# A gate row spread over partitions through DRAM instead of on TensorE, and a wait for the keys' second half moved to the third pass

## What is computed

```
mod = c_act @ w_ada[l] + b_ada[l]
shift1, scale1, gate1, shift2, scale2, gate2 = jnp.split(mod, 6, axis=-1)
...
merged = g_pool * (pooled @ w_branch_pool[l]) + g_attn * (attn @ w_branch_attn[l])
x = x + gate1[:, None, :] * (merged @ w_out[l])
h2 = modulate(x, norm_ffn_g[l], shift2, scale2)
x = x + gate2[:, None, :] * peer_ffn(h2, peer_wq[l], peer_sub_keys[l], peer_u[l], peer_v[l])
...
# second block, forgetting_attention
logits = jnp.einsum('bhqd,bhkd->bhqk', qb, k).astype(jnp.float32) * scale
logits = logits + cb[..., :, None] - cum[..., None, :]
p = jax.nn.softmax(logits, axis=-1)
```

## Time and profile before

| | us |
|---|---|
| median of 3 runs | 1173.78 |
| lowest, highest | 1173.57, 1175.6 |
| the profiled execution | 1174.26 |
| its span, first to last instruction | 1172.4 |
| PE busy | 1041.2 (89%) |
| DVE busy | 826.7 (71%) |
| ACT busy | 423.2 (36%) |
| POOL busy | 290.3 (25%) |

### The profile page before, as it was taken

How to read it: one execution, slowest core, us unless ns; L and a number is a source line. 1 busy time by engine, 2 the same in 40 slices (tenths; PEclk the granted TensorE clock), 3 DMA queues, 4 the chain that set the end, 5 groups by cost and what they waited for, 6 DMA issues and landing times.

```text
span 1172.4 us, 13740 instructions
## 1 busy us (share of the span) xinstructions
PE 1041.2 (89%) x5066; PEld 702.4 (60%) x5066; DVE 826.7 (71%) x1912; ACT 423.2 (36%) x895; POOL 290.3 (25%) x262
## 2 busy tenths in 40 slices
PE   5999999898999996886886878788899999999997
PEld 3799976644555543432332323333389878999986
DVE  5699765768767768778887555555566878888843
ACT  3545622322332222222222111111266665665631
POOL 0000001444354543353544444445000000000000
PEclk8999999999999998898988999989999999999999
DMA  9977594999999999899999999999994443554530
GB/s 367 427 319 297 239 399 158 418 401 422 420 419 420 421 422 421 365 410 421 422 421 421 422 421 422 420 422 422 384 396 180 145 179 134 198 209 163 197 144 37
DMA packets 48199, 390.46 MB, mean 333 GB/s; under 512 B 5498, under 2 KB 5890, under 8 KB 7300
## 3 DMA queue, kind: packets, MB, share of 16 engines
q0 software_dynamic: 37040, 269.51, 55.5%
q1 hardware_dynamic: 11092, 120.07, 26.1%
HBM read 388.50 MB, written 1.06 MB: 332 GB/s over the span
## 4 chain that ended last, share of the span: by engine, by line
PE 52%; DMA 31%; DVE 11%; ACT 3%; issue 2%; POOL 1%; SPq 1%; DVEq 0%
DMA ring<-in_uv,idx 27%; PE ps L1457 18%; PE ps L1801 15%; PE ps L1958 5%; DMA ring<-in_w_ada 4%; DVE ring L1243 3%; PE ps L1669 2%; PE ps L1611 2%; PE ps L1886 2%; PE ps L1481 1%; PE ps L1684 1%; DVE ring_r L885 1%; POOL ring L514 1%; PE ps L1510 1%; DVE ring L896 1%
## 5 line engine op out<-in xcount | busy, mean ns | idle before, releaser
L1801 PE MATMUL ps<-ring,probT 128*128 128x512 f32 x1020 | 490.7, 625 | 103.6 <-ACT probT L759 102.1
L1243 DVE CUSTOM_DVE_ANT_0 ring<-h2t,ring 128x1024 f32<-128x1024 f32 x255 | 308.7, 1222 | 166.0 <-DMA ring<-in_uv,idx 165.8
L1801 PEld LDWEIGHTS ps<-ring,probT 128*128 128x128 f32 x1020 | 192.6, 199 | 338.8 <-issue 194.7
L514 POOL DMA_INDIRECT ring<-in_uv,idx x255 | 287.9, 1129 | 339.1 <-PE ps L1801 287.0
L1457 PE MATMUL ps<-util_r,ring_r 128*128 128x256 f32 x1312 | 216.9, 282 | 0.0
L1457 PEld LDWEIGHTS ps<-util_r,ring_r 128*128 128x128 f32 x1312 | 181.6, 189 | 1.3 <-issue 1.1
L885 DVE TENSOR_TENSOR ring_r<-ring,ring_r 128x1024 fp32r<-128x1024 f32 x134 | 157.7, 1220 | 34.0 <-ACT ring_r L536 33.9
L754 ACT ACTIVATE prob<-prob 128x2 f32<-128x2 f32 (+2 forms) x98 | 20.0, 204 | 368.5 <-DVE prob L1243 368.4
L536 ACT ACTIVATE ring_r<-ring 128x1024 fp32r<-128x1024 f32 x134 | 133.6, 1050 | 41.5 <-DMA ring<-in_w_in 19.3
L1457 PE MATMUL ps<-h_r,ring_r 128*128 128x256 f32 x704 | 126.1, 282 | 0.1
L759 ACT ACTIVATE probT<-ct,prob 128x128 f32<-128x128 f32 x256 | 85.5, 392 | 76.5 <-DVE prob L1249 75.8
(11 more groups left out here) (213 smaller groups left out, 980.4 us busy)
## 6 DMA issues: line engine op xcount, KB each, us to landing
ring<-in_w_in SPq DMA_DIRECT2D x12, 2048.0 KB, 13.8
ring<-in_w_up SPq DMA_DIRECT2D x11, 2048.0 KB, 7.9
ring<-in_w_ada SPq DMA_DIRECT2D x7, 2048.0 KB, 9.8
ring<-in_w_down SPq DMA_DIRECT2D x6, 2048.0 KB, 7.7
ring<-in_w_ada SPq DMA_DIRECT2D x8, 1024.0 KB, 16.4
ring<-in_w_out SPq DMA_DIRECT2D x4, 2048.0 KB, 8.0
ring<-in_w_q SPq DMA_DIRECT2D x3, 2048.0 KB, 11.3
ring<-in_w_br SPq DMA_DIRECT2D x2, 2048.0 KB, 13.1
```

What stands on the lines that cost most here:

```text
L514: e.indirect_dma_start(out=row_buf[n], out_offset=None, in_=uv, in_offset=bass.IndirectOffsetOnAxis(ap=idx[:, tt, k:k + 1], axis=0)).then_inc(
L1243: e.tensor_tensor_reduce(u, h2t[:, tt, :], u, 1.0, 0.0, ALU.mult, ALU.add, av[:, tt, n % 128:n % 128 + 1]).then_inc(*made.put(("dot", n)))
L1801: ins = e.matmul(acc[half][:, :], diag[:, n % 8, :], row_buf[n][:, D + half * 512:D + (half + 1) * 512], start=(k == 0), stop=(k == 127))
```

## The change

The eight products and the two copies are gone. POOL's queue gets two transfers ahead of the gathers: when "mod2" is made, the eight columns of gate1 go to a DRAM tensor `gate_row` of 1024 numbers, in row order; when that has landed and quarter 35 is done, `gate_row` is read into all partitions. DVE's `rows_added(2, tt)` waits for this read instead of for ACT's copy. In the second block the wait of PE for the second half of the queries, and the one for the second half of the keys, move to the third pass (s = 2).

```diff
@@ gpsimd
             pool = Engine(e)
 
+            pool.wait_ge(made, "mod2")
+            e.dma_start(gate_row.rearrange("(k p) -> p k", p=P), mod[:, 16:24],
+                        allow_slow_non_contiguous=True).then_inc(*spread_gate.put("out"))
+            pool.wait_ge(spread_gate, "out")
+            pool.wait_ge(done, ("quarter", 35))
+            e.dma_start(gate1, gate_row.rearrange("(o n) -> o n", o=1).broadcast_to([P, D])).then_inc(*spread_gate.put("in"))
+
             for n in range(256):
@@ scalar
             sqrt_table(44)
-            for half in range(2):
-                act.wait_ge(done, ("gate1", half))
-                act.wait_ge(done, ("quarter", 35))
-                e.activation(gate1[:, HALF[half]], bank(("gate1", half))[:, :], ACT.Copy).then_inc(
-                    *acted.put(("gate1", half)))
@@ vector, rows_added
                         dve.wait_ge(done, ("mix1", tt, half))
-                        dve.wait_ge(acted, ("gate1", 1))
+                        dve.wait_ge(spread_gate, "in")
@@ tensor
             for z in range(4):
                 branch(0, z)
 
-            for half in range(2):
-                o = group(("gate1", half))
-                pe.wait_ge(made, "mod2")
-                for k in range(4):
-                    c = 16 + 4 * half + k
-                    ins = e.matmul(o[:, k * P:(k + 1) * P], mod[:, c:c + 1].broadcast_to([P, P]), ident, start=True,
-                                   stop=True)
-                ins.then_inc(*done.put(("gate1", half)))
-                banks.give(("gate1", half), acted, ("gate1", half))
             for z in range(4):
                 branch(1, z)
@@
-            pe.wait_ge(acted, unit("in2", 0, 2))
             pe.wait_ge(acted, unit("in2", 1, 0))
             o = group("own sums")
@@
-            pe.wait_ge(made, unit("in2", 1, 2))
             for s in range(9):
+                if s == 2:
+                    pe.wait_ge(acted, unit("in2", 0, 2))
+                    pe.wait_ge(made, unit("in2", 1, 2))
                 if s in (4, 6):
```

More of the change, by code:

```diff
@@ L214, in build @@
 def build(nc, x_in, c_in, consts, bands_in, bmask_in, cols, relb, rows, w_ada, w_in, w_pool, w_br, w_out, w_q, keysT, uv, w_in2, w_f2,
-          w_out2, w_up, w_down, out, sums):
+          w_out2, w_up, w_down, out, sums, gate_row):
     with ExitStack() as ctx:
@@ L362, in build @@
         spread_sums = Mark(sem("s_sums"), 16)
+        spread_gate = Mark(sem("s_gate1"), 16)
         stored = Mark(sem("s_stored"), 16)
@@ L368, in build @@
         made = Mark(sem("s_dve"))
-        marks = [*loaded, *half_loaded.values(), *once.values(), *arrived_in.values(), spread_sums, stored, high, low, done, acted, made]
+        marks = [*loaded, *half_loaded.values(), *once.values(), *arrived_in.values(), spread_sums, spread_gate, stored, high, low, done, acted, made]
         where = {}
@@ L2118 @@
     sums = nc.dram_tensor("sums", (8, T), F32, kind="Internal").ap()
-    build(nc, *args, out, sums)
+    gate_row = nc.dram_tensor("gate_row", (D,), F32, kind="Internal").ap()
+    build(nc, *args, out, sums, gate_row)
     r = run(nc, [arrays], core_ids=[0])
```

## The result

The changed kernel takes 1180.96 us (median of 4 runs, 1177.46 to 1182.71) against 1173.76 us before: 1.0054 times as long, with a 95% interval of 1.0028 to 1.008. It is slower by more than the 0.2% that can be told from no change, where I had forecast 1171.2 us. The profiled execution took 1177.46 us, 3.2 us more than the profiled one of before. It is the fastest of the four, so the profile shows somewhat less than the usual loss.

A forecast was written before the change was run, and what follows sets the result against it. PE was taken to set the pace at the first gate and from 895 us, saturated DMA in the gathers between. Terms -1.8 + 0.2 - 1.0 = -2.6 us gave 1171.2 us against the median, range 1169.8 to 1175.0.

The forecast's parts named there:

- the products of L1654: First gate, between the halves of L1611: removing these 8 PE products makes what follows start 1.78 us earlier.
- w + 1.26 - 1.6 - 0.5: Loss at w_out's second chunk: delay by w and the 512 KB read, less slack 1.6 and queue lull 0.5 us.
- w: Delay of the queued weights by the write of 1024 4-byte elements: between 0 and 3.5 us, taken as 1 us.
- The row came in time: Gate row for DVE's L974: write lands 148 to 158 us, read 161 to 168, before 169.7; deadline 176.5.
- The late row: Rival: write elements alternate with weight packets, read lands at 188 us, gathers 11.1 us late: 1183.9 us; chance 0.20.
- Part 2: Second block's first scores, near 895 us: moving PE's two waits to the third pass gains 1.0 us.
- The sum's first term: Loss at the merges behind the 12th ada chunk: w - 1.0, the 1.0 us being slack.
- signs of being wrong: L974 waits for a DMA; mixed() waits for w_out or a merge; or gathers start earlier but end at the same time.
- The second term: Loss at w_out's second chunk, needed by the first tile's second half: w + 1.26 - 1.6 - 0.5.
- The weights eat the gain: Rival: w of 1.8 to 3.5 us loses 1.0 to 2.7 us, ending at 1172.0 to 1173.7, same; chance 0.18.
- My formula: First gate: loss is the larger of w - 1.0 and w + 1.26 - 1.6 - 0.5, against 1.78 us gained.
- Passing on: From first gate to gathers: 1.6 us is passed on, the saturated stretch of 645 us moving as a whole.

The follow-up runs named there:

- without the write: Changed kernel without its write to DRAM, the gate read from a row of the input instead: 1171.4 us, 0.9982 of before.
- the turned row: Changed kernel with the eight columns turned into rows by one PE transpose and an ACT copy, written as 8 pieces of 512 bytes: 1171.4 us, 0.9988 of before.
- pieces apart: Changed kernel with its 1024 pieces written 512 bytes apart in DRAM, the gate read from an input row: 1172.16 us, 1.0002 of before.
- 32 bytes: Changed kernel with the same 4 KB written as 128 pieces of 32 bytes, gate values in another order: 1170.66 us, 0.9982 of before.
- part 1 alone: Kernel before with only the gate row's route through DRAM, the second block's waits left where they were: 1178.7 us, 1.0058 of before.
- the two experiments with the same write: Kernel before with only the gate's DRAM route (1178.7 us), and kernel before with only the write added, products kept (1180.17 us).
- idle queues: Kernel before with the write added only after the first queries, near 187 us, no other transfer under way: 1175.22 us; spacing and read variants 1173.56 to 1175.26.
- the write alone: Kernel before with only the write of the eight columns to DRAM added, products kept and nothing reading the row: 1180.17 us, 1.007 of before.
- 8 bytes: Changed kernel with the same 4 KB written as 512 pieces of 8 bytes, gate values in another order: 1171.83 us, 0.9992 of before.

## Why the prediction was wrong, step by step

**What was right.** PE set the pace in the gate's stretch and the products of L1654 were worth their 1.78 us: without the write, PE runs on without a gap, and counted from the start of branch(0) the first gather comes 1.8 us earlier. The read of the gate row was hidden, for about the predicted price: w_out's second chunk kept PE waiting for 0.53 us (the turned row), 0.72 (pieces apart) and 0.89 (32 bytes, PE's L1662), where the sum had w + 1.26 - 1.6 - 0.5, 0.2 us with my w. The row came in time: the write landed at 145.26 + 11.4 = 156.7 us, inside 148 to 158, and the read at 157.00 + 10.9 = 167.9, inside 161 to 168; L977's first instance, at 175.57 us, ended an idle time set by PE, as L974's had. That the write kept to its window is partly luck: the window was wide because Pool's issue was bounded by 10.2 us, which took 1.06, and with part 1 alone it landed at 145.29 + 14.4 = 159.7. The late row (the rival of 1183.9 us) did not occur; that the measured time lies inside its range is chance. Turns were not taken one piece for one weight packet, since 64 pieces share a packet. Part 2 left no idle time ahead of the scores, which is 1.0 us in the trace; the times alone (0.9992, up to 1.0001) agree with it and don't show it.

**The step that failed is w.** The cost of the write to the other transfers was bounded by 0 and 3.5 us, as 64 packets of 54 ns per engine, and I took 1. Measured on the ada chunk's landing it was 15.7 - 9.8 = 5.9 us, and 7.9 and 7.7 in the two experiments with the same write. The sum's first term, 5.9 - 1.0 = 4.9 us of loss at the merges, is nearly what happened: PE waited 5.32 us for a merge, which the prediction names among the signs of being wrong. The second term didn't bind: the second chunk of w_out was issued 4.9 us later than before (165.17 us, when DVE was done with the ada chunk), landed 8.9 us after, at 174.1, and PE needed it at 175.4. "The weights eat the gain" was the right mechanism, cut off at 3.5 us, and so without a case in which it makes the kernel slower by 0.2%.

**A term was missing too.** The sum lets PE go on at full pace after a wait. It didn't: with the granted clock at 0.50 behind the wait, mixed() took 1.8 us longer. So PE lost 5.32 + 1.84 = 7.2 us here against 1.78 gained, and counted from the start of branch(0) the first gather came 5.4 us late. It shows as 4.1 us because branch(0) began at 138.62 us in this execution and at 139.87 before, ahead of any part of the change. My formula with w = 5.9 gives max(4.9, 5.1) - 1.78 = 3.3 us; that this is near 4.1 is luck, since the missing 1.84 us and the earlier start of 1.25 us work against each other.

Why the bound was wrong: it looked for the cost where the profile has a column, in the packets' time on the DMA engines. There the write is cheap: not 64 packets on each engine but two, and 0.8% of the time. The cost arises behind the engines, where only the spacing of the pieces in DRAM matters, and the profile charges it to the weight packets: 83.0% for 1.13 MB instead of 99.7% for 3.36, 2.5 times the time per byte. A row of packets of 1 KB could not bound that from above, whatever its price per packet. The row that would have warned is the landing, and none of before had small neighbouring writes: the 8 KB copy to DRAM with its 1.6 us has 1 KB pieces.

**The rule that I weighed.** The Trainium skill, "DMA: Bandwidth & Descriptors", section "Queues, rings and completion order", puts many descriptors in a packet. The trace agrees: 64 of these pieces in one. The estimate that I drew from it was 0.6 to 4 us of waiting for weight packets. That agrees too: the write's packets of 256 bytes began 4.4 to 5.9 us after its issue in the changed kernel and 1.7 to 2.0 on idle queues, 2.7 to 3.9 us later. But it left the time of the writes themselves out, and the landing was 11.4 us. The Trainium skill's section "Rules for kernel authors", on the same page, advises against such an access because it "lowers to one descriptor per element". The advice was right for this kernel, but the number of descriptors isn't what costs here: with equally many pieces, 64 bytes apart, the write on idle queues lands in 3.5 us instead of 10.6.

**Passing on.** I took the saturated gathers to move as a whole with their start; the profiles don't bear that out to the microsecond. From first gather to last rows product the profiles show 653.0 us before, 654.2 after, 651.2 with the write alone and with part 1 alone, 656.0 without the write, with no edit in that stretch. Starts that are 4.1, 6.8 and 7.9 us late are 5.3, 5.1 and 6.2 us late at its end; a gain of 1 to 3 us at the start disappears in that scatter within one profile (without the write: 3.1 us ahead at the start, 0.1 us at the last rows product), and only medians of ten or eleven runs show it: 1.7, 2.4 and 1.6 us without the write, with 32 bytes and with the turned row.

**What stays open.** The three other runs of the changed kernel are 2.8 to 5.3 us above the profiled one. The chunk's landing varies by 2 us between the profiles of the three kernels with this write, 15.7 to 17.7, which may be part of it; the rest isn't explained. At which distance under 64 bytes the pieces begin to hurt wasn't tried. In the changed kernel 16 pieces from 16 partitions share 64 bytes of DRAM, with 8 bytes 8, with 32 bytes 2; whether their number counts, or that they come from several partitions and DMA engines, wasn't separated: these edits change both together. What in DRAM or ahead of it delays them no trace shows. That it reads back what it overwrites isn't seen: the page gives 388.50 MB read from DRAM before and with the write alone, where 1024 reads of 64 bytes would add 0.07.

## What to carry to other kernels

Don't write a column-shaped tensor to DRAM element by element, side by side, while weights that someone waits for are on the queues: turn it into rows first (one transpose and 8 pieces of 512 bytes cost next to nothing here), or leave it on TensorE, which was as fast within the noise. When a small transfer is added beside a saturated queue, look at GB/s and at the landings of its neighbours; from 150 to 158 us the DMA engines were busy for 0.85 of the time by the profile and carried a third of their bytes. A wait that a change opens on PE can cost more than its length; look at the granted clock behind it. And when bounding an unknown cost, ask at which place it could be paid (issue, engine, memory), and let the upper bound cover the places that the profile has no column for.

## What the hardware showed that I had not expected

- 1024 writes of 4 bytes side by side in 4 KB of DRAM take 10.6 us with nothing else under way, 8 us of it after the last packet has left the DMA engines; 64 or 512 bytes apart they take 3.5 and 3.4 us, and read they take 3.0 us.
- Beside weight loads this write lowers the core's whole DMA rate from 422 GB/s to 144 for eight microseconds, and the landing of a 2 MB load rises from 9.8 to 15.7 us. With the pieces 512 bytes apart the rate is 379.
- Side by side, the size of the pieces counts and not the bytes in all: 4 KB in 1024 pieces delays the chunk by 5.9 to 7.9 us, in 512 by 4.4 in the one profile (the slowest of its ten runs), in 128 and in 8 by at most 0.6.
- After PE had stood idle for 5.3 us, its granted clock was 0.50 for the next 2.7 us, and the 40 products behind the wait took 19.01 us instead of 17.17.
